# RWKV output product in two token halves, the second beside the first gathered rows; eight of 31 convolution taps as TensorE products; a ring of eleven buffers

## The reference

```
def rwkv_mix(...):
    ...
    out = (y.astype(x.dtype) * g) @ w_o
    return out, x[:, -1], s_fin

def conv_mix(x, buf, w_pw1, b_pw1, w_dw, b_dw, ln_g, ln_b, w_pw2, b_pw2):
    h = x @ w_pw1 + b_pw1
    u = h[..., :D] * jax.nn.sigmoid(h[..., D:])
    full = jnp.concatenate([buf.astype(u.dtype), u], axis=1)
    c = lax.conv_general_dilated(full, w_dw[:, None, :], window_strides=(1,), ...) + b_dw
    ...   # layer norm over the channels
    out = jax.nn.silu(cn) @ w_pw2 + b_pw2

def peer(x, w_q, sub_keys, u_tab, v_tab):
    ...   # q = x @ w_q, two top-16 lists, the best 16 of their 256 sums
    act = jax.nn.gelu(jnp.einsum('bhkd,bd->bhk', u_tab[idx], xb), approximate=False)
    return jnp.einsum('bhk,bhkd->bd', gate * act, v_tab[idx])
```

## Time and profile before

| | us |
|---|---|
| median of 3 runs (4190.53 to 4209.57) | 4191.19 |
| the profiled execution's own time | 4196.97 |
| its span in the trace | 4195.2 |
| `w_o` product, first to last product | 936.4 to 1001.1 |
| first gather issued | 1033.8 |
| chunks of cA, first taps | 1803.8 to 2193.6 |
| chunks of cB, first taps | 2680.8 to 3011.7 |

### The profile page before, as it was taken

How to read it: one execution, slowest core, us unless ns; L and a number is a source line. 1 busy time by engine, 2 the same in 40 slices (tenths; PEclk the granted TensorE clock), 3 DMA queues, 4 the chain that set the end, 5 groups by cost and what they waited for, 6 DMA issues and landing times.

```text
span 4195.2 us, 42635 instructions
## 1 busy us (share of the span) xinstructions
PE 3525.0 (84%) x12440; PEld 1962.3 (47%) x12440; DVE 2866.3 (68%) x6575; ACT 1480.4 (35%) x4136; POOL 1482.4 (35%) x1272
## 2 busy tenths in 40 slices
PE   5999999987888888898887977988799887777776
PEld 3777777766443333344443533444345333333332
DVE  5444444443766666789997777899977677777775
ACT  1233333321433333443344433423244333333333
POOL 0111111111444444444443454333334444444442
PEclk8899999999999999999998999998899999999999
DMA  2000000002999999999999999998989999999996
GB/s 76 22 22 22 22 22 22 17 13 99 427 427 426 427 427 427 426 423 394 406 413 405 394 427 425 424 337 321 331 342 376 427 425 426 427 427 427 427 427 293
DMA packets 228382, 1305.21 MB, mean 311 GB/s; under 512 B 58608, under 2 KB 61808, under 8 KB 80496
## 3 DMA queue, kind: packets, MB, share of 16 engines
q0 software_dynamic: 165888, 1208.03, 69.5%
q1 hardware_dynamic: 62320, 95.24, 6.5%
HBM read 1297.32 MB, written 5.86 MB: 311 GB/s over the span
## 4 chain that ended last, share of the span: by engine, by line
DMA 27%; DVE 21%; PE 19%; ACT 3%; issue 2%; DVEq 2%; POOL 1%; ACTq 0%; POOLq 0%
DMA arena<-in_uv,arena 27%; PE psum L1136 13%; DVE arena L1532 10%; DVE arena L1609 5%; PE psum L1100 4%; PE psum L1224 2%; POOL arena L1080 1%; DVE arena L1587 1%; ACT wbuf L1333 1%; DVE arena L1460 1%; DVEq L1611 1%; PE psum L1147 0%; DVE arena L1457 0%; ACT arena L1328 0%; DVE arena L1590 0%
## 5 line engine op out<-in xcount | busy, mean ns | idle before, releaser
L1136 PE MATMUL psum<-arena,wbuf 128*128 128x512 f32 (+1 forms) x4608 | 2120.8, 638 | 512.8 <-ACT wbuf L1333 511.3
L1080 POOL DMA_INDIRECT arena<-in_uv,arena x1152 | 1354.1, 1175 | 1792.0 <-PE psum L1136 1680.7
L1532 DVE SCALAR_TENSOR_TENSOR arena<-arena 128x1024 f32<-128x1024 f32 x1152 | 1396.8, 1223 | 544.2 <-DMA arena<-in_uv,arena 524.5
L1136 PEld LDWEIGHTS psum<-arena,wbuf 128*128 128x128 f32 (+1 forms) x4608 | 810.8, 193 | 1638.0 <-ACT wbuf L1333 825.9
L1324 ACT ACTIVATE arena<-arena 128x2 f32<-128x2 f32 x576 | 117.0, 203 | 1735.1 <-DVE arena L1532 1734.4
L1333 ACT ACTIVATE wbuf<-cst,arena 128x128 f32<-128x128 f32 (+1 forms) x1152 | 392.9, 388 | 41.4 <-issue 1.4
L1100 PE MATMUL psum<-arena,wbuf 128*128 128x256 f32 (+1 forms) x1024 | 287.8, 427 | 8.5 <-DVE arena L1543 5.8
L1328 ACT ACTIVATE arena<-arena 128x1 f32<-128x1 f32 x1152 | 276.7, 287 | 40.4 <-issue 0.7
L1100 PEld LDWEIGHTS psum<-arena,wbuf 128*128 128x128 f32 x1024 | 202.1, 200 | 129.1 <-issue 88.8
L1609 DVE SCALAR_TENSOR_TENSOR arena<-arena,par 128x256 f32<-128x256 f32 x480 | 232.0, 483 | 22.3 <-issue 1.0
L846 POOL COPY arena<-arena 128x256 f32<-128x256 f32 x8 | 3.2, 396 | 655.5 <-DVE arena L744 655.5
(11 more groups left out here) (252 smaller groups left out, 3327.4 us busy)
## 6 DMA issues: line engine op xcount, KB each, us to landing
wbuf<-in_w_q SPq DMA_DIRECT2D x64, 576.0 KB, 8.9
arena<-in_w_pw SPq DMA_DIRECT2D x48, 512.0 KB, 9.7
arena<-in_uv,arena POOLq DMA_INDIRECT x1152, 21.6
wbuf<-in_w_rkv SPq DMA_DIRECT2D x24, 512.0 KB, 3.5
wbuf<-in_w_o SPq DMA_DIRECT2D x8, 512.0 KB, 3.6
x<-in_x SPq DMA_DIRECT2D x1, 2304.0 KB, 8.1
arena<-in_state SPq DMA_DIRECT2D x16, 128.0 KB, 2.9
out_o_wkv_s<-arena SPq DMA_DIRECT2D x16, 128.0 KB, 2.6
```

The costliest lines, as they stand in the source:

```text
L1080: pool.indirect_dma_start(ring[:, g % RING, :], None, I["uv"][p // 2], bass.IndirectOffsetOnAxis(ap=idx[:, s % 4, j:j + 1], axis=0)).then_ ...
L1136: last = pe.matmul(out, diag[:, g % DIAGS, 0:P if u < NB else NS], ring[:, g % RING, D + e * 512:D + (e + 1) * 512], start=head == 0 and j ...
L1532: stt(out=row, in0=row, scalar=1.0, in1=tok[p % 2][:, UNITS[p % 2].index(u), :], op0=ALU.mult, op1=ALU.mult, accum_out=dots[:, g % RING:g ...
```

## The change

- `linear_into_x` is gone. The product with `w_o` is made in two parts by a new generator `linear`, which the convolution's output product uses as well. Part "wA" (half 0, 256 columns) stands at the start of the last block, ahead of the norm and the first queries. Part "wB" (half 1, 320 columns) is background work of phase 0, from row 4, three rows for each of 8 chunks, with the weights loaded again into the background buffers `wb` (`output_loads`). The norm of half 1 moves from row 6 to 32, its transposition to tokens from 30 to 46.
- `wkv` writes y as two tensors, one for each half, so its last multiply is two instructions.
- Of the 31 taps of the 256 prompt columns, taps 0 to 7 go to TensorE. ScalarE makes eight diagonal matrices of tap weights (128 x 128) for each chunk, TensorE adds diagonal times shifted `up` in a PSUM area `part` (bank 5 in cA, 6 in cB), and ScalarE copies the sum with the bias to `cv` ("tap_sum"). VectorE waits for that at the chunk's row 5 and adds taps 8 to 30 in the remaining rows; the taps of the new tokens now come ahead of them. The next chunk's projection starts 3 rows into the chunk instead of 0, and its part in the shared bank waits for tap_sum.
- The ring has 11 buffers instead of 12; the small columns (`dots`, `gelu`, `coef`) stay 12 (COLS). The diagonals take the freed space.

```diff
-    RING, DIAGS, LEAD = 12, 8, 2
+    RING, DIAGS, LEAD, COLS = 11, 8, 2, 12
+    PE_TAPS = 8
...
         if p == 0:
-            return dict(norm=6, tok=30)
+            return dict(linear=4, norm=4 + 3 * C + 4, tok=4 + 3 * C + 18)
...
+            def output_loads(t):
+                for c in range(C):
+                    if c >= 2:
+                        yield from tick.until(t["linear"] + 3 * (c - 2) + 4)
+                        sp.wait_ge(pe_b.sem, pe_b.value(f"wB.product{c - 2}"))
+                    sp.dma_start(wb[c % 2], I["w_o"][c]).then_inc(bl[c % 2], 16)
...
+            for c in range(2, C):
+                sp.wait_ge(pe_b.sem, pe_b.value(f"wA.product{c - 2}"))
+                sp.dma_start(K.w[c % 2], I["w_o"][c]).then_inc(wo_loaded[c % 2], 16)
             load_query(0)
...
+            def linear(n, half, at, src, weights, loaded, before):
+
+                for c in range(C):
+                    yield from tick.until(at + 3 * c)
+                    if c >= 2:
+                        pe.wait_ge(dve_b.sem, dve_b.value(f"{n}.into_x{c - 2}"))
+                    pe.wait_ge(loaded[c % 2], 16 * (before + c // 2) + 16)
+                    for k in range(C):
+                        yield from tick.until(at + 3 * c + k // 4)
+                        last = pe.matmul(ps[:, BANK[c % 2], 0:WIDTH[half]], weights[c % 2][:, k, :], src[:, k, :],
+                                         start=k == 0, stop=k == C - 1)
+                    last.then_inc(pe_b.at(f"{n}.product{c}"), 1)
...
+                        if j == half and c:
+                            yield from tick.until(at + 2)
+                            pe.wait_ge(act_b.sem, act_b.value(f"{n}.tap_sum{c - 1}"))
...
+                def taps(c, at):
+                    pe.wait_ge(act_b.sem, act_b.value(f"{n}.diags{c}"))
+                    pe.wait_ge(dve_b.sem, dve_b.value(f"{n}.glu{c}"))
+                    for k in range(PE_TAPS):
+                        yield from tick.until(at + k // 4)
+                        last = pe.matmul(part, tap_diags[:, k, :], ups[c % 2][:, k:k + 2 * P], start=k == 0, stop=k == PE_TAPS - 1)
+                    last.then_inc(pe_b.at(f"{n}.tapped{c}"), 1)
...
+                    yield from taps(c, at)
                     if c < C - 1:
-                        yield from project(c + 1, at)
+                        yield from project(c + 1, at + 3)
...
+                    at = t["conv"] + (c - 1) * t["chunk"]
+                    for k in range(PE_TAPS):
+                        yield from tick.until(t["project"] if c == 0 else at + 5 + k // 2)
+                        if k == 0 and c:
+                            act.wait_ge(pe_b.sem, pe_b.value(f"{n}.tapped{c - 1}"))
+                        last = act.activation(tap_diags[:, k, :], K.ident, ACT.Copy, scale=K.par[:, TAP0 + k, c:c + 1])
+                    last.then_inc(act_b.at(f"{n}.diags{c}"), 1)
...
+                    yield from tick.until(at + t["chunk"] + 4)
+                    act.wait_ge(pe_b.sem, pe_b.value(f"{n}.tapped{c}"))
+                    act.activation(cv[half][:, c, 0:2 * P], part, ACT.Identity,
+                                   bias=K.par[:, B_DW, c:c + 1]).then_inc(act_b.at(f"{n}.tap_sum{c}"), 1)
...
+                    yield from tick.until(at + 5)
+                    dve.wait_ge(act_b.sem, act_b.value(f"{n}.tap_sum{c}"))
+                    spread = t["chunk"] - 6
+                    for k in range(PE_TAPS, TAPS):
+                        yield from tick.until(at + 5 + (k - PE_TAPS) * spread // (TAPS - PE_TAPS))
+                        last = stt(out=out, in0=up[:, k:k + 2 * P], scalar=K.par[:, TAP0 + k, c:c + 1], in1=out, op0=ALU.mult, op1=ALU.add)
```

150 lines of the change are left out of this document (59 added, 91 removed), and 1 row of the table TASKS.

## The result

The changed kernel takes 4149.85 us (median of 4 runs, 4145.0 to 4153.6) against 4192.27 for the kernel before (4 runs, 4190.53 to 4209.57): a ratio of 0.9898, 95% interval 0.9881 to 0.9915, 42 us or 1.0% less. The profiled execution took 4145.0 us, its span is 4143.2. The forecast was 4147.

The account below looks back on a forecast made before the run. VectorE was taken to bound both convolutions and the gather stream (DMA) the rows outside them. The terms, -34 + 10 + 6 - 10 - 21 + 5 = -44, gave 4147 us by the median; range 4115 to 4181.

Parts of the forecast that it names:

- Term 1: Output product ahead of the first gather: only 64 of 256 columns stay in front, -34 us (-31 to -37).
- Term 2: Half 1's output product beside the gathered rows: +10 us for rereading the weight, +6 for TensorE falling behind.
- the twin's rows: Output product of half 1's convolution, same shape, 9.46 us for 3 rows; used to forecast TensorE falling 10.7 us behind.
- Term 3, taps in cA: Convolution beside half 0: eight taps moved from VectorE to TensorE, -10 us for eight chunks (-20 to 0).
- three within 4%: Half 0's convolution: forecast chunk times of VectorE 54.2 us, DMA 53.2 and TensorE 52.0, close together.
- Term 3, taps in cB: Convolution beside half 1: eight taps moved from VectorE to TensorE, -21 us (-34 to 0).
- the 16 that were to show: Sign: VectorE's first tap, at row 5, follows idle time released by ScalarE, 16 times, near 2 us each.
- Term 4: Ring of eleven buffers: run-ahead lost at the convolution's two output products, +5 us (0 to 8).
- (a): Rival: half 1's product is hidden by the ring and VectorE's wait is covered, -78, 4113 us; chance 0.15.
- (b): Rival: the taps give nothing because TensorE is full, -13, 4178 us; chance 0.18.
- (c): Rival: TensorE lags its rows, so VectorE waits 7.5 us a chunk for the partial sum, +40, 4231 us; chance 0.08.
- (d): Rival: half 1's product is not hidden at all, while the taps gain as forecast, -16, 4175 us; chance 0.07.

Follow-up runs that it names:

- halves_only: Kernel before with only the output product in halves, all 31 taps on VectorE and a ring of twelve; 4166.4 us, ratio 0.9935.
- product_every5: Changed kernel with half 1's output product taken one chunk every five rows instead of every three; 4150.04 us, ratio 0.9899.
- own_first: Changed kernel, VectorE starting its taps at row 1 and adding TensorE's sum from PSUM itself, half 0's next projection at row 6; 4137.78 us, ratio 0.9867.
- one_tap_product: Changed kernel with seven of the eight TensorE tap products of each chunk left out; 4144.41 us, ratio 0.9888.
- late_wait: Changed kernel with VectorE waiting for the sum and starting its own taps at row 7 instead of 5, both halves; 4146.11 us, ratio 0.9881.
- ring11_only: Kernel before with 11 ring buffers instead of 12, nothing else; 4196.97 us, ratio 1.0013.

## Why the prediction was right, point by point

**The sum.** Forecast -44 against the profiled execution of before; measured -52, of which -7.9 is RWKV, whose code changed by one split multiply, and -44.1 the rest, which is the change's. By the medians, 4149.85 against 4192.27, it is -42. The mechanism forecast is the one seen in the front and in cB. That the total agrees to a microsecond is luck: 7.8 us that cA's taps did not give are made up by 7.1 that product and ring cost less than their 16 + 5, and 2.4 that cB with its eighth chunk gave beyond its 21; "between" takes 1.2 back and the front 0.4.

**Term 1, the front, -34: right.** -33.6 in the pair, -33.8 in halves_only. The eight products took 33.2 and not 31.5 us, probably in part because the loads land after 3.7 us instead of 3.4; the way from the last product to the first gather is 1.7 us shorter (30.8 against 32.6) where 1.1 was forecast, which paid for some of it. First gather at 992.3, forecast "near 1000".

**Term 2, half 1's product, +16: right in size, wrong in its parts.** +13.9 in the pair, 781.0 - 768.2 = +12.8 for the mean of six. The failed step is "9.8 us of DMA ... with no cover": with 7.2 us of it taken away nothing came back. TensorE's excess (10.7 us behind, by the twin's rows) is the binding one, and the second reading hides in it. The two should have been taken as the larger of the two with a remainder, not as a sum. The rate of 423 to 425 GB/s that the forecast named as its sign was there, and would have misled: a full queue doesn't say that the transfers bind. Nor does a full TensorE: it is busy 50.00 of 50 us in product_every5 as well, where taking the loads away did give 4.4 us.

**Term 3, taps in cA, -10: wrong.** -2.2 in the pair, -0.7 for the mean of the five against the mean of the three with 31 taps (390.1). Two steps failed. "DMA alone would need 408 x 55.7 / 427 = 53.2" took the floor from bytes; the shortest chunk of any kernel is 54.4, which leaves 1.3 us a chunk and not 2.5. Whether that is the floor of the transfers (54.3 by share) or TensorE's part in the chain stays open. And of the gain taken, 1.2 a chunk, nearly nothing came: the sum over a chunk didn't see that VectorE's taps now begin at row 5, so that it has too little to do ahead of them and too much behind. The wait itself was forecast well, 8 x 2.7 = 21.6 us against 20.2 (1.94 to 4.36 each). own_first gets 8.7 us of it back. Taking VectorE as the last of "three within 4%" was right for before; in after the chain through cA is TensorE's for half.

**Term 3, taps in cB, -21: right.** -20.6 over seven chunks, 2.9 each, which is 23.5 over eight. Forecast was the full 3.0 less a reserve of 0.3 for TensorE. The waits were six and sum to 10.0 us, forecast 1.2 a chunk, 9.6 in all; with cA's eight that makes 14 of the 16 that were to show. The reserve wasn't needed: one_tap_product shows that TensorE binds nothing there. By the rule of the Trainium skill, Perfetto Trace Analysis, section Identifying the Most-Contended Engine, that TensorE's headroom is read from weight loads and not from matmul busy time, the term was -24; the measured 23.5 is on its side. In cA loads are busy 186.88 of 387.6 us, 48%, and there TensorE was on the path all the same. The bound of -34, no wait at all, is where late_wait comes to, 8 x (47.6 - 43.5) = -33: VectorE has next to no wait left there, and its own work, 47.3 - 4.2 = 43.1 us by the forecast's terms, is the chunk. The floor of 38.0 that the forecast wrote down is too low by the queues (39.9 to 43.5), but bound nothing.

**Term 4, the ring, +5: wrong place, about the right size.** Nothing at the convolution's output products (ring11_only, +0.3 in all); likely some 3 us beside half 1's product.

**The rivals.** (a), all hidden, 4113: half 1's product isn't hidden, and no kernel got more than 9 us out of cA. (b), taps give nothing: true of cA, false of cB. (c), a wait of 7.5 us a chunk: the waits were 2.5 on average in cA and 4.4 at most. (d), the product not hidden at all: 13.9 of 44. Chunk starts were forecast 54.5 and 44.6 apart; measured 55.4 and 44.7.
